# Two-layer hybrid trunk: twelve of sixteen modulation kinds summed on VectorE, six of them inside FFN input stretches

## The reference

```python
mod = (jax.nn.silu(c_ctx) @ w_mod[l] + b_mod[l]).reshape(1, 1, 3 * N_SUB, D_MODEL)
...
def modulated(j, y):
    return _rmsnorm(y, g[j]) * (1 + mod[:, :, 3 * j + 1]) + mod[:, :, 3 * j]
x = x + 0.5 * mod[:, :, 2] * _swiglu(modulated(0, x), ffn_w_in[l, 0], ffn_w_out[l, 0])
h = modulated(1, x)
...
x = x + mod[:, :, 5] * out
x = x + 0.5 * mod[:, :, 8] * _swiglu(modulated(2, x), ffn_w_in[l, 1], ffn_w_out[l, 1])
```

## Time and profile before

| | |
|---|---|
| median of three runs | 2393.9 us (2392.03 to 2394.64) |
| the profiled execution | 2396.54 us, span 2394.7 us |
| granted clock, mean over the span | 0.994 |
| busy: TensorE, VectorE, ScalarE | 98%, 66%, 41% |
| DMA | 251.61 MB, 105 GB/s in the mean |
| loads of grains, time to landing | 128 of 512 KB, 6.0 us in the median |
| loads of FFN input weights, time to landing | 176 of 512 KB, 4.9 us in the median |

### The profile page before, as it was taken

The page is one execution under the profiler, slowest core; times in us unless marked ns, Lnnn a source line. Parts: engine busy times, 40 slices in busy tenths (PEclk is TensorE's granted clock), DMA queues, the critical chain, the costliest instruction groups (busy, mean ns, idle before and its releaser), DMA issues.

```text
span 2394.7 us, 39770 instructions
## 1 busy us (share of the span) xinstructions
PE 2340.2 (98%) x16652; PEld 2263.6 (95%) x16652; DVE 1568.7 (66%) x2366; ACT 973.1 (41%) x1545; POOL 0.2 (0%) x4
## 2 busy tenths in 40 slices
PE   7999999999989999999999999999999999999999
PEld 6999999989769999999999999999999999999998
DVE  4886776657766876677587767676245768467463
ACT  6533423354556433414374243245215364334142
POOL 0000000000000000000000000000000000000000
PEclk9999999999999999999999999999999999999999
DMA  8342544322101252434224344333221012322132
GB/s 293 124 146 94 193 149 166 132 72 63 47 19 54 89 159 89 141 124 141 89 72 174 108 156 152 115 111 99 88 71 45 19 54 71 106 71 89 53 97 71
DMA packets 201420, 251.61 MB, mean 105 GB/s; under 512 B 12994, under 2 KB 178074, under 8 KB 201242
## 3 DMA queue, kind: packets, MB, share of 16 engines
q1 hardware_dynamic: 201242, 249.07, 31.8%
HBM read 245.76 MB, written 3.28 MB: 104 GB/s over the span
## 4 chain that ended last, share of the span: by engine, by line
PE 84%; DVE 6%; ACT 4%; DMA 3%; issue 3%; SPq 0%; DVEq 0%; ACTq 0%
PE banks L1052 72%; DMA w_raw<-ffn_w_in 2%; DVE w_lo L2476 2%; ACT w_hi L1906 1%; PE banks L1199 1%; DVE w_raw L2497 1%; PE banks L1390 1%; PE banks L1392 1%; PE banks L1391 1%; PE banks L1477 1%; PE banks L1489 1%; DVE hid_lo L2754 1%; ACT prob L2278 0%; PE banks L1504 0%; PE banks L1670 0%
## 5 line engine op out<-in xcount | busy, mean ns | idle before, releaser
L1052 PE MATMUL banks<-b_hi,w_hi 128*128 128x320 f32 x2496 | 779.3, 312 | 15.6 <-DVE b_lo L2654 7.9
L1052 PE MATMUL banks<-b_hi,w_lo 128*128 128x320 f32 x2496 | 772.8, 310 | 0.0
L1052 PE MATMUL banks<-b_lo,w_hi 128*128 128x320 f32 x2496 | 772.8, 310 | 0.0
L1052 PEld LDWEIGHTS banks<-b_hi,w_hi 128*128 128x128 f32 x2496 | 469.9, 188 | 35.3 <-issue 23.2
L1906 ACT ACTIVATE w_hi<-w_raw 128x1024 fp32r<-128x1024 f32 x296 | 310.3, 1055 | 416.8 <-PE banks L1052 235.9
L2476 DVE TENSOR_TENSOR w_lo<-w_raw,w_hi 128x1024 fp32r<-128x1024 f32 x296 | 361.5, 1223 | 171.7 <-ACT w_hi L1906 170.1
L1052 PEld LDWEIGHTS banks<-b_lo,w_hi 128*128 128x128 f32 x2496 | 470.1, 188 | 0.0
L1052 PEld LDWEIGHTS banks<-b_hi,w_lo 128*128 128x128 f32 x2496 | 470.0, 188 | 0.0
L1052 PE MATMUL banks<-hid_hi,w_hi 128*128 128x320 f32 x1664 | 397.0, 311 | 3.0 <-DVE hid_lo L2754 1.5
L1052 PE MATMUL banks<-hid_lo,w_hi 128*128 128x320 f32 x1664 | 394.1, 309 | 0.0
L1052 PE MATMUL banks<-hid_hi,w_lo 128*128 128x320 f32 x1664 | 394.0, 309 | 0.0
(11 more groups left out here) (326 smaller groups left out, 2550.6 us busy)
## 6 DMA issues: line engine op xcount, KB each, us to landing
w_raw<-ffn_w_in SPq DMA_DIRECT2D x176, 512.0 KB, 4.9
mod_grain<-w_mod SPq DMA_DIRECT2D x84, 512.0 KB, 6.0
w_raw<-ffn_w_out SPq DMA_DIRECT2D x64, 512.0 KB, 4.5
last_grain<-w_mod SPq DMA_DIRECT2D x44, 512.0 KB, 6.0
w_raw<-ffn_w_out SPq DMA_DIRECT2D x32, 384.0 KB, 3.8
w_raw<-w_in_odd SPq DMA_DIRECT2D x20, 512.0 KB, 4.8
mod_first<-w_mod SPq DMA_DIRECT2D x3, 2048.0 KB, 15.8
w_raw<-w_in_even SPq DMA_DIRECT2D x12, 512.0 KB, 5.0
```

The costliest lines, as they stand in the source:

```text
L1052: ins = pe.matmul(o, w3[w], v3[v][cols], start=first and i == 0, stop=last and i == 2, skip_group_check=onto_read)
```

## The change

Six more kinds are summed by VectorE: 4, 6, 10, 12, 14 and 16 are added inside doubles 4 to 7 and 8 to 10 of FFN 0, 1 and 2 (`ADDED_IN`). Four, four, four and four operations fall to doubles 4 to 7, and five, five and six to doubles 8 to 10 (`DOUBLE_OPS`). Their places in a double are five slots (`SLOT_OPS`): behind split 4, behind split 5, between the two L2768 additions, behind split 0 of the next double, and between the two L2805 additions. The kinds 3, 5, 9, 11, 13 and 15 stay in the output stretches (`ADDED_OUT`), and 2, 7, 8 and 17 are made by products, in windows of doubles 1 to 3. Before, ten kinds were made by products (twenty windows) and six by adding; now four (eight windows) and twelve. The kinds are done in a new order (`KIND_ORDER`), and what was counted by a kind's number is counted by its place in it.

The sum product of an inner kind stands behind product 6 of double 7 or 10, and its keeping behind the low parts of the hidden tiles and of output unit 3. `clear_ss` moves behind it. SP loads an inner kind's grains between the loads of weights.

```diff
+        WINDOWS = ({(1, 4): (2, 0), (2, 1): (2, 1), (3, 1): (7, 0), (3, 4): (7, 1)}, {(2, 4): (8, 0), (3, 4): (8, 1)},
+                   {(2, 4): (17, 0), (3, 4): (17, 1)}, {})
+        ADDED_OUT = ({0: 3, 1: 5}, {0: 9, 1: 11}, {0: 13, 1: 15}, {})
+        ADDED_IN = ({1: 4, 2: 6}, {1: 10, 2: 12}, {1: 14, 2: 16}, {})
+        SUMS = [{**{(doubles_until(c), 1): kind for c, kind in ADDED_OUT[f].items()},
+                 **{(doubles_until(c) - 1, ITEMS - 1): kind for c, kind in ADDED_IN[f].items()}} for f in range(4)]
         ADD_OPS = (3, 3, 3, 3, 2, 1, 0, 1)
+        DOUBLE_OPS = {1: (4, 4, 4, 4), 2: (5, 5, 6)}
+        SLOT_OPS = {4: (0, 1, 1, 2, 0), 5: (1, 1, 1, 2, 0), 6: (1, 1, 1, 2, 1)}
...
+        def ops_before(f, d):
+
+            c = chunk_of(d)
+            return sum(DOUBLE_OPS[c][:d - CHUNK_PARTS * c]) if c in ADDED_IN[f] else 0
...
+                    inner, outer = ADDED_IN[f].get(c), ADDED_OUT[f].get(c) if last else None
+                    done = ops_before(f, d)
+                    ready = done + DOUBLE_OPS[c][d - CHUNK_PARTS * c] if inner is not None else None
                     if last:
                         load_out(f, c, 0)
+                    else:
+                        load_in(f, d + 1, 0)
+                    if inner is not None and done // 2 + 2 < (ready + 1) // 2:
+                        load_grain(inner, done // 2 + 2)
+                    if last:
                         load_out(f, c, 1)
                     else:
                         load_in(f, d + 1, 1)
+                        if inner is not None:
+                            for kt in range(max(done // 2 + 2, (ready + 1) // 2), min(ready // 2 + 2, KT)):
+                                load_grain(inner, kt)
...
+                def add_slot(i):
+
+                    if c in ADDED_IN[f]:
+                        slots = SLOT_OPS[DOUBLE_OPS[c][d - CHUNK_PARTS * c]]
+                        add_grains(ADDED_IN[f][c], ops_before(f, d) + sum(slots[:i]), slots[i])
+
                 item_lo(f, d, 4)
+                add_slot(0)
...
                 item_lo(f, d, 5)
+                add_slot(1)
...
                 for s in range(2):
                     add_p2(f, d, s)
+                    if s == 0:
+                        add_slot(2)
                 item_lo(f, d, 6)
                 if not last and d > 1:
                     item_lo(f, d + 1, 0)
+                add_slot(3)
                 for s in range(2):
+                    if s == 1:
+                        add_slot(4)
                     dve.wait_ge(u2_kept, done + s + 1)
...
-                if kind_done is not None:
+                if kind_done is not None and kind_done not in ADDED_IN[f].values():
                     keep_kind(kind_done)
-                if last and c == len(CHUNKS) - 1:
-                    clear_ss()
...
                 if last:
                     out_lo(f, c, 2)
                     out_lo(f, c, 3)
+                    if c in ADDED_IN[f]:
+                        keep_kind(kind_done)
+                    if c == len(CHUNKS) - 1:
+                        clear_ss()
```

49 lines of the change are left out of this document (24 added, 25 removed), and 3 rows, old and new, of the table WINDOWS.

## The result

The change makes the kernel slower. Five runs of the changed kernel have a median of 2408.8 us (2406.0 to 2410.3), five of the kernel before 2393.6 us (2391.4 to 2394.6), 15.2 us apart. The ratio on record is 1.0057, 95% interval 1.0046 to 1.0068, which is 13.6 us on 2393.6. The prediction was 2409.8 us. The profiled execution took 2407.3 us (span 2405.5), against 2396.5 us (span 2394.7) before: the spans differ by 10.8 us. The profiled execution before was slower than all five of those runs, so what the two traces differ by is 4.4 us less than the medians do.

What follows compares the result with a forecast made beforehand. It took TensorE as bound, with VectorE's path through the split of product 6 and the weight transfer close behind. Stalls of 35.7 less 17.5 and 2.3 gave +15.9 us: 2409.8 us against the median, range 2390 to 2424.

Steps and rivals of the forecast that it cites:

- first sum: VectorE's weight sum at L2497 behind the two L2805 additions; needs the next double's second weight half; TensorE follows 4.03 us behind.
- rival 2: Weight transfer is quicker alone, so the next product's split decides; stalls 21.6 us in all, result 2395.7 us; chance 0.13.
- TensorE's 17.5 us: Net TensorE gain: twelve product windows fewer save 24.6 us, six sum products more cost 7.1 us.
- the 2.3 us of old waits: Earlier TensorE stalls that go: 0.8 us in double 5 of FFN 1, and 0.49 us three times for hid_lo.
- The longer way to split 6: VectorE, first sum to split of product 6: 19.53 us with two early additions; keeping adds 1.39 in doubles 5 and 9.
- The transfer, 7.20 us: Load of the next weights' second half, from start of the split of product 6 to the first sum: 7.20 us.
- The 6.7 us set aside for a shared transfer: Grains sharing DMA engines with weights: up to 0.74 us in nine doubles, 6.7 us, kept out of the sum.
- Doubles 4, 8 and 10: TensorE stalls expected in each FFN: 0.8 us in double 4, the same in double 8, 0.6 us in double 10.
- SP and late grains, priced at nothing: Grain loads waiting on SP for VectorE's additions between weight loads cost nothing; a late grain would hold VectorE's following work.
- Rival 3: TensorE's clock falls behind new gaps in doubles 5, 6 and 9; 8.4 us more, 2418.2 us; chance 0.10.
- the sign set for being right: Doubles 5, 6, 9: TensorE waits 2 us or more on L2815; first sums 26 to 29 us apart, ending in DMA waits.
- rival 1: The additions fit VectorE's waits and TensorE loses nothing; 17.5 + 2.3 us gained, 2374.1 us; chance 0.16.

Runs made afterwards that it cites:

- the kernel with all moves: Changed kernel, twelve kinds still by additions, with the keeping earlier and additions redistributed, more of them behind the split of product 6: 2387.1 us, ratio 0.9961.
- The grains' bytes taken away: Changed kernel with each inner kind's grain transfer bringing 8 columns of 1,024, every VectorE operation kept in place: 2408.9 us, ratio 1.0050.

## Why the prediction was right

**Reading of the bound: right.** A first sum that ends in the wait for its weights, and TensorE right behind it, is what the timeline after and the cut of the late additions show. What the reading missed is that the part behind split 6 is not empty of deadlines. The split of the next product 0 starts a second chain, and its slack is smaller than the 2 x 1.20 us that stand there. The prediction used that chain only for doubles 4 and 8 and for rival 2. Priced alone, it would have told that taking away the early pair gives back a third of what it seems to cost.

**TensorE's 17.5 us and the 2.3 us of old waits: right.** The terms can be read on TensorE directly. A double without a window, sum or wait takes 24.64 us; double 5 of FFN 2, with one window, took 26.70 before (2.06 more), and double 4 with a sum product 25.83 in the kernel with all moves (1.19 more). The total is less sharp: with the additions cut it is 18.4 us by the two profiles, once the remaining waits are taken out, and 15.9 by the ratio, give or take 3.6. The wait of 0.49 us for the low part of the hidden values is gone in the three last chunks.

**The longer way to split 6: right.** The 19.53 us and the 1.39 of the keeping make 20.92 from first sum to split 6 in double 5; FFN 0 has 20.91.

**The transfer, 7.20 us: too high.** Split 6 to first sum took 6.62 to 6.94 us in doubles 5, 6 and 9, with the additions behind it cut 6.6 to 7.1, and 6.74 with the grains' bytes gone. That is the main part of the difference in chunk 1: spacing 27.56 to 27.70 us in double 5 against 28.12, 28.4 to 28.7 in double 9 against 28.86, 26.2 to 26.7 in double 6 against 26.73. The 6.7 us set aside for a shared transfer did not come in this kernel; where a grain stood closer before the second half, 0.8 us and more did ("The grains' bytes taken away"). By the fit in the Trainium skill's "DMA: Bandwidth & Descriptors" (Anatomy of one DMA) an estimate for the transfer is shorter still, 5.6 us from the start of the split; these rows lie between that and the 7.20, and nearer to the latter. The section gives its fit for transfers issued by GpSimd, and here SP issues them, so the difference does not test it.

**Doubles 4, 8 and 10: too high by little.** Doubles 4 and 8 lost 0.5 us (two waits of 0.24 and 0.27) against 0.8. Double 10 showed no wait against 0.6, but the half clock behind double 9 hid a part: it took TensorE 25.73 us, and 26.07 with the keeping moved ahead, where the clock held.

**Stages.** The forecast's 107.4 and 82 us take in two sum products each. Up to the first output unit, and so with the second of them, chunk 1 took 106.9, 106.3 and 106.9 us, chunk 2 82.0, 83.0 and 82.2. The six together are some 567 us against 568.2. So the stalls, with what the clock lost, come to 35 us, as in the sum. Without what the clock lost in double 9 they would come to some 29.

**SP and late grains, priced at nothing: right for this change**, with 4.3 us of idle time, nearly all for grains, in front of 168 multiply-adds, but it has a price that depends on the place: ahead of split 0 the same grain cost 4.28 us once.

**The clock, left out of the sum: wrong, and hidden.** Rival 3 happened in five of six places, and in double 6 it worked as described there: TensorE at half clock needs so long that it only just waits for VectorE (0.24 and 0.26 us in FFNs 0 and 2), where I had 2.06 us of stall. So the size of double 6 was right by the wrong cause in two FFNs; FFN 1, whose clock held, had the waits instead (0.76 and 0.27 us). So the sign set for being right, waits of 2 us and more in doubles 5, 6 and 9, showed in 5 and 9 only, and in double 6 of FFNs 0 and 2 the first sum did not wait for its DMA either. Of double 9's loss most remains on top: 1.7, 3.4 and 1.7 us, less the 0.3 us that double 10 would have lost at full clock. The rival's number, 2418, was too high, since no gap arose in double 6 for the clock to fall behind, and the stalls themselves were smaller. The pattern that the Trainium skill's "TensorE: Matmul & The Clock Gate" (HAM oscillation) describes, waits between bursts of matmuls and a lower clock behind them, did arise. The waits in that section's case are of some 3 to 5 us; here the clock fell behind gaps from 1.9 us on.

**Rivals 1 and 2.** That the additions fit is false as they were placed. With them placed otherwise it is nearly true for doubles 4 to 7, as rival 1 put it: the additions must not move the transfer. Rival 2 had the direction of the transfer right, but the chain through split 0, on which it relied, is longer than it assumed: with the early additions cut, double 5 still needed 26.9 to 27.8 us.

So the mechanism is right in its main part and the closeness of the total is luck. Three misses cancel: a transfer 0.4 us too long in three doubles of each FFN, small stalls that did not come, and a clock loss of some 6 us net that was not in it. Nor does every measure agree as well: 15.9 us were forecast, and the medians differ by 15.2, the ratio gives 13.6 and the two traces 10.8. In the traces doubles 4 to 10 of FFN 0 to 2 grew by 7.3 us and the rest of the kernel by 3.5.
